# Weights of a transformer block cast from device memory to device memory instead of into on-chip memory and back, with the second tile's input, positions and masks issued later

## The reference

```
x <- x + 1/2 * SwiGLU_1(RMSNorm(x))                       # 1024 -> 2816 -> 1024
h  = RMSNorm(x)
[glu_a | glu_b | q | k | v | g_conv | g_attn] = h @ w_in
conv = (silu(LayerNorm(causal_dwconv31(glu_a * sigmoid(glu_b))))) @ conv_w_proj
attn = sliding_window_attention(rope(q), rope(k), v, sinks) @ w_o    # window 128, 16 heads, 4 kv heads
x <- x + (sigmoid(g_conv) * conv + sigmoid(g_attn) * attn) @ w_out
x <- x + 1/2 * SwiGLU_2(RMSNorm(x))
out = RMSNorm_final(x)
```

## Time and profile before

| | |
|---|---|
| median of 3 runs | 1955.47 us (1954.86 to 1959.61) |
| the profiled execution: its time, and its span from first to last instruction | 1954.62 us, 1953.6 us (core 6; the other cores 1937.2 to 1950.1 us) |
| TensorE busy | 1706.7 us, 87% of the span |
| DVE, ACT, POOL busy | 800.8, 710.2, 705.8 us |
| mean granted TensorE clock, core 6 / die 0 / die 1 | 0.928 / 0.939 / 0.933 |
| moved by the DMA engines | 315.44 MB, mean 161 GB/s; HBM read 300.80 MB, written 67.37 MB |

### The profile page before, as it was taken

How to read it: one execution, slowest core, us unless ns; L and a number is a source line. 1 busy time by engine, 2 the same in 40 slices (tenths; PEclk the granted TensorE clock), 3 DMA queues, 4 the chain that set the end, 5 groups by cost and what they waited for, 6 DMA issues and landing times.

```text
span 1953.6 us, 30366 instructions; the slowest of 8 cores (1937.2 to 1953.6 us)
## 1 busy us (share of the span) xinstructions
PE 1706.7 (87%) x9316; PEld 768.7 (39%) x9316; DVE 800.8 (41%) x1305; ACT 710.2 (36%) x1460; POOL 705.8 (36%) x608
## 2 busy tenths in 40 slices
PE   2998777799996798799999899959999998999897
PEld 1554333243442343344443344424443343444343
DVE  1431313746424248554114347462213448643312
ACT  2211213545312136553322246464312237632231
POOL 1102126434431267441323256324323257432231
PEclk9998887788997999899999999959999999999898
DMA  9999797235896889677443853434443752345423
GB/s 235 198 203 207 187 199 202 69 103 108 182 207 180 210 208 194 184 177 236 154 149 122 212 166 135 130 108 151 139 152 125 192 175 98 124 127 163 137 93 119
DMA packets 120493, 315.44 MB, mean 161 GB/s; under 512 B 14352, under 2 KB 36112, under 8 KB 120336
## 3 DMA queue, kind: packets, MB, share of 16 engines
q1 hardware_dynamic: 102368, 257.72, 42.6%
q0 software_dynamic: 17424, 54.73, 18.3%
q10 hardware_dynamic: 544, 1.05, 0.2%
HBM read 300.80 MB, written 67.37 MB: 188 GB/s over the span
## 4 chain that ended last, share of the span: by engine, by line
PE 69%; DMA 15%; DVE 6%; issue 4%; ACT 2%; SPq 2%; POOL 1%; DVEq 0%; ACTq 0%; POOLq 0%
PE ps L485 64%; PE ps L82 4%; DMA wac<-wa 3%; DMA ush<-uT 2%; SPq L98 2%; DMA wa<-wall 2%; DMA RR<-ush 2%; DVE sm L82 2%; DMA cvo<-xT 2%; DMA ush<-S 1%; DMA wdc<-wd 1%; DVE S L82 1%; PE ps L673 1%; DVE X L82 1%; POOL P L82 1%
## 5 line engine op out<-in xcount | busy, mean ns | idle before, releaser
L485 PE MATMUL ps<-xnF,wa 128*128 128x512 bf16 x2816 | 665.5, 393 | 36.8 <-DVE tf L82 13.6
L485 PEld LDWEIGHTS ps<-xnF,wa 128*128 128x128 bf16 x2816 | 274.1, 100 | 390.3 <-issue 129.2
L485 PE MATMUL ps<-Hh,wd 128*128 128x512 bf16 x1408 | 331.3, 384 | 9.8 <-DMA wd<-wd 9.3
L485 PE MATMUL ps<-xnM,wa 128*128 128x512 bf16 x1344 | 325.9, 393 | 12.3 <-DVE xnM L82 10.9
L82 ACT ACTIVATE tf<-ps 128x512 f32<-128x512 f32 x304 | 178.4, 595 | 297.6 <-PE ps L485 276.9
L82 POOL TENSOR_TENSOR Hh<-tf 128x512 bf16<-128x512 f32 x128 | 163.6, 1280 | 231.8 <-PE ps L485 117.1
L82 DVE SCALAR_TENSOR_TENSOR tf<-tf,ps 128x512 f32<-128x512 f32 x176 | 120.5, 685 | 273.4 <-PE ps L485 256.7
L485 PEld LDWEIGHTS ps<-xnM,wa 128*128 128x128 bf16 x1344 | 132.5, 100 | 195.0 <-issue 58.8
L485 PEld LDWEIGHTS ps<-Hh,wd 128*128 128x128 bf16 x1408 | 135.8, 99 | 175.6 <-issue 24.7
L82 ACT ACTIVATE S<-S,sm 128x256 f32<-128x256 f32 x256 | 129.5, 506 | 87.7 <-DVE sm L82 72.4
L82 POOL TENSOR_TENSOR P<-S,sm 128x1024 bf16<-128x1024 f32 x64 | 121.7, 1903 | 104.4 <-DVE sm L82 63.4
(11 more groups left out here) (101 smaller groups left out, 1687.2 us busy)
## 6 DMA issues: line engine op xcount, KB each, us to landing
wa<-wac SPq DMA_DIRECT2D x234, 512.0 KB, 3.5
wa<-wall POOLq DMA_DIRECT2D x78, 512.0 KB, 9.3
wac<-wa SPq DMA_DIRECT2D x78, 512.0 KB, 8.7
wd<-wdc SPq DMA_DIRECT2D x96, 352.0 KB, 3.1
RR<-ush SPq DMA_DIRECT2D x128, 135.0 KB, 4.2
wd<-wd POOLq DMA_DIRECT2D x32, 352.0 KB, 9.3
wdc<-wd SPq DMA_DIRECT2D x32, 352.0 KB, 7.3
outT<-X SPq DMA_DIRECT2D x16, 512.0 KB, 5.5
```

Of the source, the lines that this page charges most:

```text
L485: op(PE, lambda: mm(out, lhsT=pick(use.slot), rhs=rhs, start=start, stop=stop), rd, wr, t, use)
```

## The change

`_store` is gone. At a block's first use the weights no longer go float32 to slot to copy; `_cast` on POOL casts them from device memory into the bf16 copy in device memory (`wac<-wall`, `wdc<-wd`), planned at least `AHEAD` = 40 us ahead of the use, and SP loads the copy into the slot like at every later use. Two blocks alone (`direct` = 2) are still cast into their slots, and are cast a second time into their copies, planned at 100 us. A casting transfer waits for the one 16 places ahead of it (16 semaphores `s_cast`) and, for `SA`, lists tile 0's last input chunk as read (`gate`). At the start `misc` and `cols` come first, and `load_x(1)`, the positions and `ident` list an `H_b` entry as read, a buffer that the first FFN writes. The planner's numbers for `ush` and `RR` transfers go from 4 and 6 to 5 and 9 us, which can move convolution work in all four tiles.

```diff
+AHEAD = 40.0
@@ class Stream
-    def events(self):
+    def events(self, ahead):
         out = []
-        held = {}
+        done = set()
         for j, u in enumerate(self.uses):
             s = j % self.depth
             u.slot, u.buf = self.slots[s], self.bufs[s]
-            out.append((self.issue[j] + 0.001, 1, lambda j=j, u=u, s=s: self._load(j, u, s, held)))
-            if u.key not in held and self.seen[u.key] > 1:
-                out.append((min(u.at + 0.5, u.end), 0, lambda u=u, s=s: self._store(u, s, held)))
-                held[u.key] = None
-        held.clear()
+            out.append((self.issue[j] + 0.001, 1, lambda j=j, u=u, s=s: self._load(j, u, s)))
+            if u.key not in done:
+                done.add(u.key)
+                at = min(u.at - ahead, self.issue[j] - 12.0) if j >= self.direct else 100.0 + j
+                out.append((max(0.0, at), 0, lambda u=u: self._cast(u)))
         return out
...
-    def _load(self, j, u, s, held):
-        if u.key in held:
-            src = self.cache(u.key)
-            emit_dma(self.hq, self.hsems[s], [(self._view(s, src), src)], (held[u.key],), (self.bufs[s],))
-        else:
+    def _load(self, j, u, s):
+        if j < self.direct:
             src = self.src(u.key)
             emit_dma(self.q, self.sems[s], [(self._view(s, src), src)], (), (self.bufs[s],))
-
-    def _store(self, u, s, held):
-        dst = self.cache(u.key)
-        held[u.key] = Buf()
-        emit_dma(self.hq, self.ssems[s], [(dst, self._view(s, dst))], (self.bufs[s],), (held[u.key],))
+        else:
+            src = self.cache(u.key)
+            emit_dma(self.hq, self.hsems[s], [(self._view(s, src), src)], (self.held[u.key],), (self.bufs[s],))
+
+    def _cast(self, u):
+        self.held[u.key] = Buf()
+        sem = self.chan[1][self.chan[2] % len(self.chan[1])]
+        self.chan[2] += 1
+        emit_dma(self.q, sem, [(self.cache(u.key), self.src(u.key))], self.gate, (self.held[u.key],))
@@ build_nc
-        chan = [0.0]
-        SA = Stream(chan, POOL, SP, [w[:] for w in wa], wa_b, wa_s, wa_ss, wa_hs, asrc, acache, [0.0, 0.0, 0.0, 14.0, 18.0, 22.0], (5.1, 1.6))
-        SD = Stream(chan, POOL, SP, [w[:] for w in wdd], wd_b, wd_s, wd_ss, wd_hs, dsrc, dcache, [60.0, 66.0, 72.0, 78.0, 84.0], (3.5, 1.1))
+        chan = [0.0, [mksem(f"s_cast{i}") for i in range(16)], 0]
+        SA = Stream(chan, POOL, SP, [w[:] for w in wa], wa_b, wa_s, wa_hs, asrc, acache, [0.0, 0.0, 16.0, 18.0, 20.0, 22.0], (5.1, 1.6), 2, (X_b[0][7],))
+        SD = Stream(chan, POOL, SP, [w[:] for w in wdd], wd_b, None, wd_hs, dsrc, dcache, [60.0, 66.0, 72.0, 78.0, 84.0], (3.5, 1.1), 0, ())
...
-                dma(SP, sem, [(ush_d[cc][:, c0:c0 + N], u_t)], rd=(u_b,), wr=(db,), t=4.0)
+                dma(SP, sem, [(ush_d[cc][:, c0:c0 + N], u_t)], rd=(u_b,), wr=(db,), t=5.0)
...
-                rd=(ush_b[cc], ushh_b[cc]), wr=(RR_b[cc % NRR],), t=6.0)
+                rd=(ush_b[cc], ushh_b[cc]), wr=(RR_b[cc % NRR],), t=9.0)
...
+        cdma(SP, "misc", misc[:], misc_d, misc_b)
+        cdma(ACT, "cols", cols[:], cols_d, cols_b)
         load_x(0)
-        cdma(SP, "misc", misc[:], misc_d, misc_b)
-        cdma(SP, "cols", cols[:], cols_d, cols_b)
-        dma(SP, s_xh, [(Xh, xT_d[:, 0:HALO].rearrange("(c p) t -> p c t", p=128))], wr=Xh_b)
+        dma(SP, s_xh, [(Xh, xT_d[:, 0:HALO].rearrange("(c p) t -> p c t", p=128))], wr=Xh_b, t=20.0)
...
-        load_x(1)
-        load_pos(0, HALO, cos_h, cosh_b)
-        load_pos(HALO, NT, cos_t, cos_b)
-        cdma(POOL, "ident", ident[:], ident_d, ident_b)
+        load_pos(0, HALO, cos_h, cosh_b, (H_b[6],))
+        load_pos(HALO, NT, cos_t, cos_b, (H_b[6],))
+        cdma(POOL, "ident", ident[:], ident_d, ident_b, (H_b[9],))
         cdma(POOL, "pswap", pswap[:], pswap_d, pswap_b)
         cdma(POOL, "masks", masks[:], masks_d, masks_b)
+        load_x(1, (H_b[16],))
```

More of the change, by code:

```diff
@@ L226, with __init__ @@
 class Stream:
-    def __init__(self, chan, q, hq, slots, bufs, sems, ssems, hsems, src, cache, first, occ):
-        self.first, self.occ = first, occ
-        self.chan = chan
+    def __init__(self, chan, q, hq, slots, bufs, sems, hsems, src, cache, first, occ, direct, gate):
+        self.chan, self.first, self.occ, self.direct, self.gate = chan, first, occ, direct, gate
         self.q, self.hq, self.slots, self.bufs = q, hq, slots, bufs
-        self.sems, self.ssems, self.hsems, self.src, self.cache = sems, ssems, hsems, src, cache
+        self.sems, self.hsems, self.src, self.cache = sems, hsems, src, cache
         self.depth = len(slots)
@@ L236, in __init__ @@
         self.issue = []
+        self.held = {}
     def use(self, key, who="F"):
@@ L298, in emit @@
     for st in streams:
-        events += st.events()
+        events += st.events(AHEAD)
     events.sort(key=lambda v: v[:2])
@@ L377, in build_nc @@
         wa_s = [mksem(f"s_wa{i}") for i in range(NA)]
-        wa_ss = [mksem(f"s_was{i}") for i in range(NA)]
         wa_hs = [mksem(f"s_wah{i}") for i in range(NA)]
@@ L381, in build_nc @@
         wdd = [sb(f"wd{i}", [128, 11, 128], BF16) for i in range(ND)]; wd_b = bufs(ND)
-        wd_s = [mksem(f"s_wd{i}") for i in range(ND)]
-        wd_ss = [mksem(f"s_wds{i}") for i in range(ND)]
         wd_hs = [mksem(f"s_wdh{i}") for i in range(ND)]
@@ L426, in build_nc, with cdma @@
         b8 = Banks(every)
-        def cdma(q, name, dst, src, buf):
-            dma(q, mksem("s_c_" + name), [(dst, src)], wr=(buf,))
+        def cdma(q, name, dst, src, buf, after=()):
+            dma(q, mksem("s_c_" + name), [(dst, src)], rd=after, wr=(buf,))
         def alias(news, olds):
@@ L485, in MMW, with load_x @@
             op(PE, lambda: mm(out, lhsT=pick(use.slot), rhs=rhs, start=start, stop=stop), rd, wr, t, use)
-        def load_x(t):
+        def load_x(t, after=()):
             b0 = HALO + t * NT
@@ L491, in load_x @@
                     [(X[t % 2][:, 2 * h:2 * h + 2, :], xT_d[256 * h:256 * h + 256, b0:b0 + NT].rearrange("(c p) t -> p c t", p=128))],
-                    wr=X_b[t % 2][2 * h:2 * h + 2], t=8.0)
+                    rd=after, wr=X_b[t % 2][2 * h:2 * h + 2], t=8.0)
         def proj(pst, pb, use, sub, rhs_t, rhs_bufs, N):
@@ L619, in f_b, with load_pos @@
                                     x_t[:, 2 * h:2 * h + 2, :])], rd=x_bufs[2 * h:2 * h + 2], t=8.0)
-        def load_pos(base, N, c_t, c_b):
-            dma(SP, s_pos[N == NT], [(c_t[:, 0:N].bitcast(I32), pos_d[:, base:base + N])], wr=(c_b,))
+        def load_pos(base, N, c_t, c_b, after=()):
+            dma(SP, s_pos[N == NT], [(c_t[:, 0:N].bitcast(I32), pos_d[:, base:base + N])], rd=after, wr=(c_b,))
         def rope_tables(N, c_t, c_b, s_t, s_b):
```

## The result

The changed kernel took 2207.56 us, median of 4; before took 1955.37 beside it. Two of the four executions (2298.18 and 2346.24) had one die at a lower clock; by the other two (2115.83 and 2116.95) the ratio to before is 1.082 [1.079, 1.084]. That is **slower by 160 us**, outside my range (1892 to 1978) and against my likeliest sign. The profiled execution has a span of 2115.9.

A forecast was written before the change was run, and what follows sets the result against it. Tile 0's first FFN (0 to 205 us) was taken as bound by transfers. Terms 13 - 12 - 24 - 8 - 7 + 8 = -30 on 1954.6 us gave 1925 us; range 1905 to 1942, with most of B and C 1892 to 1978.

The forecast's parts named there:

- First FFN, +13: Tile 0's first FFN: more cast and plain-queue bytes, casts priced at 6.63 us per written MB, cost 13 us.
- Mixer, -12: Tile 0's mixer: same megabytes and DMA share; half of the 23.9 us of convolution read-back waits go, 12 us saved.
- POOL, -24: Casts no longer wait for slots, so TensorE's waits of 16.0 and 7.6 us behind POOL go, 24 us saved.
- Convolution, -8: Tiles 1 to 3: a third of the 11.0 and 11.9 us of convolution waits goes through new planning, 8 us saved.
- New waits, +8: Loads on SP waiting for casts or slots hold the convolution's transfers behind them; cost 8 us (0 to 20).
- Clock, -7: TensorE's clock after waits and between 221 and 317 us: half the 13.6 us loss goes, 7 us saved.
- Start, 0: Kernel start: TensorE's first projection at 37 us against 40.6, worth 0 while transfers bound the stage.
- A: Rival: casts within device memory are dear; 1983 us at 9.5 us per MB, likeliest 1955; chance 0.20.
- B: Rival: long cast pieces hold up loads in tile 0's first FFN, which ends 60 us later; 1980 us; chance 0.17.
- C: Rival: casts within device memory are cheap, 5.8 us per MB, first FFN ends earlier; 1888 us; chance 0.13.
- D: Rival: another wait fills POOL's holes, so the 24 us of waits stay; 1949 us; chance 0.08.

The follow-up runs named there:

- e15: Changed kernel with short cast pieces, the input ahead of the casts, the identity matrix's wait removed and two casts in flight, all together; 1.0688 of before.
- e10: Kernel before, with the new method (cast ahead within device memory, then load) for the mixer's weight blocks alone; 1.0264 of before.
- e8: Kernel before, with the new method (cast ahead within device memory, then load) for the second feed-forward block's weights alone; 1.0163 of before.
- e6: Kernel before, with only the planner's numbers for the shifted copy changed (5 us for `ush`, 9 us for `RR`); 1.0045 of before.
- e2: Changed kernel with casts planned at 1 us or later, so tile 0's input is issued before them; 1.0888 of before.
- e4: Kernel before, with only the new start and its held-back transfers, weights handled as before; 1.0017 of before.
- e11: Nine phases of transfers alone in place of the kernel's work, on 8 cores; casts took 6.4 us per MB into slots, 9.4 within device memory.
- e1: Changed kernel with padded copies in device memory, so a cast is 128 rows of 2048 elements instead of 16 pieces of 16384; 1.0788 of before.
- e17: Kernel before, with a plain 0.49 MB copy within device memory, which nothing waits for, behind each weight block's store; 1.1457 of before.
- e7: Changed kernel with the identity matrix's cast no longer waiting for the tenth block of hidden values (`H_b[9]`); 1.0979 of before.

## Why the prediction was wrong

**First FFN, +13.** This step failed. It took 108.6. "I take 6.63, since the cast is the same on its reading side": measured 9.4 alone and 8.5 in the stage (60.2% of 314 us for 22.22 MB). My upper bound, "a cast plus a store, 9.5", was the right value. By queue: casts 189.0 us instead of 135.1 (+54), plain transfers 89.2 instead of 60.9 (+28, where I had 6), and about 30 us in which the engines were not busy instead of 4 (+26). 24 of these lie between 260 and 314 us: the last load for the up projections came at 250, when the casts were through, and from then on TensorE worked without a hole while the engines were only 0.55 busy. Before, the down projections ran from 144 us on beside full engines. In e15, where loads landed earlier (12.2 us), the engines were idle for about 12 us. That loads wait for casts where stores could lag is my explanation of this; no run takes that wait alone away. The 24.2 MB I counted on the plain queues were right (24.60 on SP's and 1.09 on ACT's, with five early loads of `wd`, 1.8 MB, among them); their price was not: 3.63 us per MB instead of 2.89.

**Mixer, -12, "the same megabytes, so the DMA share … stays".** Wrong in the same way: I counted written bytes. For each MB written, a cast into a slot is two MB of traffic at device memory (its reads) and a cast into a copy three; the store of one MB became a read-back of one MB. Alone this part costs 52 us (e10).

**POOL, -24.** Right for these waits, in place and size: `acc` and `P` together fell from 59.4 to 35.6 us. In tile 1 no wait for a sum was over 5 us, and none of POOL's nine largest waits from 420 to 1000 us is for a transfer. But from 420 to 860 us 46.6 us of waits for `wa<-wac` came, so that no time was won, and e8 shows the exchange.

**Convolution, -8.** `RR`'s waits fell by 4.4 us in all (42.4 for 46.8), of the 20 of both terms. The numbers alone won 9.9 us there and no time (e6).

**New waits, +8.** The largest error beside the first: 179.0 us for `wa<-wac` and 15.2 for `wd<-wdc`, over all tiles. They are how the lost DMA time reaches TensorE, not a cost of its own.

**Clock, -7.** No gain. Over the first block it went the other way: after TensorE's new holes the granted clock was 0.84 instead of 0.97 on average between the levels of 1.2 and 2.4 GHz, and the same 1072 matmuls took 168.1 us for 157.0. Over the whole span TensorE's busy time hardly changed (1703.5 us for 1706.7), so the clock accounts for next to nothing of the 160 us.

**Start, 0.** TensorE's first projection came at 48.27 us, not 37; that it is worth nothing held (e2, e4).

**The rivals.** A is in the main what happened, at its dear end and beyond: 9.4 us per MB and falling GB/s at full share. My 1983 for that end was too low, since I priced A in the first block alone and left the mixer and the second FFN at no cost, and because dearer plain transfers and idle engines came on top. B's signature was there (landing 46.2 us, holes early), and e11 shows the mechanism; but e1 and e15 show that it carries little of the time. It decides who waits, and of the stage's length only a small part. C is out (9.4 for its 5.8 us per MB). D's exchange of one wait for another is what e8 shows in tile 1, at a price and not at nothing.

## What to carry to other kernels

Count a stage's transfers by what device memory reads and writes, not by what the queue writes; that fits every phase measured here. A copy made within device memory is read, written and read back, and "ahead of use" doesn't hide it where the DMA engines are already 0.98 busy. Before moving a transfer, ask whether its stage is full; if so, nearly every MB there shows (the four mends of the order got back a sixth), and moving it to the next stage helps only as far as that one has room. A transfer that can lag, like a store, seems to cost less than one that something waits for: 106 us more of queue time put e17's block back by 106 us, 82 us more put the changed kernel's back by 109.

## What was not expected of the hardware

Six casts in long pieces in flight (e11, phase 6) left a plain queue of 512 KB loads 10.4% of the engines' time (78.7 us to land instead of 9.3), while the sum of both was no longer than the two one after the other. And taking an 88 us wait off POOL made the kernel 1.6 points slower (e7).
